# Up-projection weight loads of a mixture-of-experts stage moved from SyncE's queue to ScalarE's queue

## The chip, the cores and the metric

The kernel runs on one core of one Trainium2 chip. The metric is the device time of one execution in microseconds (us). Engines are named as in the profile: PE (TensorE), PEld (its weight loads), DVE (VectorE), ACT (ScalarE), POOL (GpSimd) and SP (SyncE). An engine's name with a q (SPq) means its sequencer, which issues DMA instructions. The core has 16 DMA engines, and every queue uses all of them.

## The reference, cut to what matters

One inference step of a two-layer hybrid decoder on 264 tokens (256 of a prompt, 8 of decoding), all in float32. Each layer first mixes tokens (pooling, differential attention, a state space), then runs a mixture of experts. For this change only the experts matter:

```
scores = sigmoid(t @ w_r)                      # 264 tokens, 64 experts, the best 8 per token
for each of 64 experts (wg, wu: 1024 x 256; wd: 256 x 1024; 1 MB each):
    a = silu(t @ wg) * (t @ wu)
    acc += gate[:, None] * (a @ wd)
shared = (silu(t @ sg) * (t @ su)) @ sd
```

## The kernel before, in words

**Tiling.** Before the expert loop the kernel sorts each expert's tokens into blocks of 64. Every expert has one block, and 32 spare blocks take the tokens beyond 64 of crowded experts. The loop has 96 steps: after every second expert comes one spare block. So 64 steps use weights whose address is known when the program is built ("main" steps), and 32 use weights that are found by an index ("spare" steps, numbers 2, 5, 8, 11 and so on). Spare blocks that no expert needs have an index out of bounds, and then no weights are read.

**Buffers.** Gate and up weights of a step share one slot `raw[n % 5]` of 2 MB, one half each. Down weights have 4 slots `dn`, the gathered token rows `xg` 4 buffers, the output rows `ytok` 4 buffers. A main step's gate, up and down loads have 1 MB each, in rows of 8 KB, and the semaphore of a slot counts 16 for each half.

**Order by engine in step n.** No planner is at work; each engine has a program written by hand, and semaphores tie them together.

- PE: `gate_up(n)` (line 1263, 32 matmuls), `turn_x(n+1)` (line 879, transposes of the gathered rows `xg`), `down(n-1)` (line 1276), `turn_act(n)` (line 879, input `scratch`). `turn_x` waits for the gather of its step.
- ACT: `copy_x(n+1)` (line 1474) moves the transposed rows out of PSUM, then it waits for `gu_made` of step n (the end of `gate_up(n)`), then silu (line 1498).
- DVE: the product with the up half (line 1853), the copy of the output rows (line 1859), the copy of the transposed activation (line 1863).
- SP: `gate_up(m)` waits until step m-5 has left the slot, then issues the gate half and the up half (line 642, one after the other); then `down(m-2)` waits for its slot and issues the down weights (line 657). Spare steps are skipped.
- POOL: waits for `turn_x(n+1)`, issues the gather of step n+4 (line 821); in a spare step's turn its gate and up loads (line 834); then waits for the output rows of step n-1, issues their scatter (line 828), and in a spare step's turn the down load (line 834). At n = 8 and 9 it also sends a small table to memory and back (`sgate`, `gflat`, line 696) and waits for the first of these to land. All that POOL issues goes through one queue, in order.

Of the kernel before, what the change touches and what calls it, by code (L numbers as in the profile page):

```python
# [25 lines left out]
P = 128  # L26
# [22 lines left out]
NE, TOPK, NG, TOPG = 64, 8, 8, 4  # L49
# [23 lines left out]
STEPS = [b for e in range(NE) for b in ([e, NE + e // 2] if e % 2 == 1 else [e])]  # L73
assert NE // 2 == SPARE and sorted(STEPS) == list(range(BLOCKS))
NSTEP = len(STEPS)
NRAW, NDOWN, NX, NY = 5, 4, 4, 4
# [117 lines left out]
def program(nc, a, out):  # L194
# [12 lines left out]
    def placed(name, of, first, shape, dt):  # L207

        return nc.alloc_sbuf_tensor_at(name, shape, dt, offset=places[of] + 4 * first)
# [4 lines left out]
    def sig(name, per_layer):  # L214
        return Signal(sem(name), per_layer)
# [123 lines left out]
    raw = [placed(f"raw{n}", of, first, [P, 2, SEG], F32) for n, (of, first) in enumerate(raw_at)]  # L339
# [132 lines left out]
    raw_loaded = [sig(f"raw_loaded{r}", 32 * len(MAIN_RAW[r])) for r in range(NRAW)]  # L472
# [58 lines left out]
    def _(sp):  # L531
        def columns(w, s):
            return w[:, 256 * s:256 * s + 256].rearrange("(k p) n -> p k n", p=P)

        def seg(t):
            return t.rearrange("p (k n) -> p k n", k=KD)
# [49 lines left out]
        def wide_fill(layer, f):  # L586
            ada, win = a["w_ada"][layer], a["w_in"][layer]
            if f < ADA_FIRST:
                w, s = ada, 2 * f
            elif f < ADA_FIRST + WIDE_IN:  # L590
                w, s = win, 2 * (f - ADA_FIRST)
            else:
                w, s = ada, 2 * (f - WIDE_IN)
            sp.wait_ge(wide_free, layer * WIDE_FILLS + f + 1)
            for j in range(2):
                sp.dma_start(seg(wide[:, f % 2, j]), columns(w, s + j)).then_inc(wide_loaded[f % 2], 16)
# [11 lines left out]
        for layer in range(DEPTH):  # L608
            wout = a["w_out"][layer]
            for f in range(0 if layer == 0 else 2, WIDE_OUT):  # L610
                if f == 2:
                    load_parameters(layer)
                wide_fill(layer, f)
            sp.wait_ge(wide_free, layer * WIDE_FILLS + WIDE_OUT + 1)
            for j in range(2):
                sp.dma_start(seg(wide[:, WIDE_OUT % 2, 0])[:, 4 * j:4 * j + 4],
                             columns(wout, 0)[:, 4 * j:4 * j + 4]).then_inc(wide_loaded[WIDE_OUT % 2], 16)
            for f in range(NARROW_SHARED):
                sp.wait_ge(narrow_free, layer * NARROW_FILLS + f + 1)
                sp.dma_start(seg(narrow[:, f % 2]), columns(wout, f + 1)).then_inc(narrow_loaded[f % 2], 16)  # L620

            sp.wait_ge(wide_free, layer * WIDE_FILLS + WIDE_SHARED + 1)
            for j, name in enumerate(("shared_w_gate", "shared_w_up")):
                sp.dma_start(seg(wide[:, 1, j]), a[name][layer].rearrange("(k p) n -> p k n", p=P)).then_inc(wide_loaded[1], 16)

            def gate_up(n):
                b = STEPS[n]
                if n == 0:
                    sp.wait_ge(attn_mixed.sem, attn_mixed.by(layer, 1))
                elif n == 1:  # L630
                    sp.wait_ge(ada_late.sem, ada_late.by(layer, WIDE_ADA - ADA_FIRST))
                    sp.wait_ge(ssm_mixed.sem, ssm_mixed.by(layer, 1))
                elif n == 2:
                    sp.wait_ge(out_first_used.sem, out_first_used.by(layer, 1))
                elif n == 3:
                    sp.wait_ge(hrows_stored.sem, hrows_stored.by(layer, 48))
                elif n == 4:
                    sp.wait_ge(sh_made.sem, sh_made.by(layer, 2))
                else:
                    sp.wait_ge(gu_made.sem, gu_made.by(layer, n - NRAW + 1))  # L640
                for j, name in enumerate(("exp_w_gate", "exp_w_up")):
                    sp.dma_start(raw[n % NRAW][:, j], a[name][layer, b].rearrange("(p k) n -> p (k n)", p=P))\
                        .then_inc(raw_loaded[n % NRAW].sem, 16)

            def down(n):
                b = STEPS[n]
                if n == 0:
                    sp.wait_ge(out_last_used.sem, out_last_used.by(layer, 1))
                elif n == 1:
                    sp.wait_ge(out_made.sem, out_made.by(layer, KD))  # L650
                elif n == 2:
                    sp.wait_ge(sh_down.sem, sh_down.by(layer, KD))
                elif n == 3:
                    sp.wait_ge(sh_made.sem, sh_made.by(layer, 2))
                else:
                    sp.wait_ge(down_made.sem, down_made.by(layer, n - NDOWN + 1))
                sp.dma_start(dn[n % NDOWN][:, :, :].rearrange("p j n -> p (j n)"),
                             a["exp_w_down"][layer, b].rearrange("(p j) n -> p (j n)", p=P))\
                    .then_inc(down_loaded[n % NDOWN].sem, 16)

            for n in range(NSTEP + 2):
                if n < NSTEP and STEPS[n] < NE:
                    gate_up(n)
                if n == 1:
                    sp.wait_ge(narrow_free, layer * NARROW_FILLS + NARROW_SHARED + 1)
                    sp.dma_start(narrow[:, 1].rearrange("p (k n) -> p k n", k=2),
                                 a["shared_w_down"][layer].rearrange("(k p) n -> p k n", p=P)).then_inc(narrow_loaded[1], 16)
                if n >= 2 and STEPS[n - 2] < NE:
                    down(n - 2)

            if layer + 1 < DEPTH:
                for f in range(2):
                    wide_fill(layer + 1, f)
            for r in range(NY):
                sp.wait_ge(y_scattered[r].sem, y_scattered[r].by(layer + 1, 0))
            ytok_k = yrows_k.rearrange("(t k) n -> t k n", k=TOPK)
            for g in range(4):
                for t in range(2):
                    sp.dma_start(ypart[t][g // 2][:, 2 * (g % 2):2 * (g % 2) + 2, :],
                                 ytok_k[P * t:P * t + P, 2 * g:2 * g + 2, :]).then_inc(y_loaded[g].sem, 16)  # L680
            sp.dma_start(ysam[:, :], yrows_k[TOPK * NP_:TOPK * T, :]).then_inc(ysam_loaded.sem, 16)

        yrows = projT[:, :, :].rearrange("p a b -> p (a b)")[:, 0:3 * D].rearrange("p (a b) -> p a b", a=3)
        for t in range(3):
            sp.wait_ge(last["copied"], 2 * t + 2)
            dst, n = (out["y_prompt"][0, P * t:P * t + P, :], P) if t < 2 else (out["y_sample"][:, 0, :], NS)
# [634 lines left out]
    def _(se):  # L1321
# [10 lines left out]
        for layer in range(DEPTH):  # L1332

            def W(s, k=1):
                se.wait_ge(s.sem, s.by(layer, k))
# [36 lines left out]
            for c in range(0, PROJ, 2):  # L1372
                W(proj_made, c + 1)
                act_(projT[:, c, :], ps[:, c % 4, 0:T], ACT.Copy).then_inc(proj_copied_a.sem, 1)
                if c % 4 == 2:

                    p = c // 4
# [9 lines left out]
            for n in range(4):  # L1387
                m = 512 if n < 3 else 256
# [79 lines left out]
            def copy_x(n):  # L1468
                W(x_turned, n + 1)
                if n == 0:  # L1470
                    W(table_made, 3)
                elif n >= 2:
                    W(gu_made, n - 1)
                act_(xTs[n % 2][:, :, :].rearrange("p k r -> p (k r)"), ps[:, n % 2, :], ACT.Copy).then_inc(x_copied.sem, 1)  # L1474
# [3 lines left out]
            for t in range(3):  # L1478
                n = P if t < 2 else NS
# [14 lines left out]
            for n in range(NSTEP):  # L1494
                if n + 1 < NSTEP:
                    copy_x(n + 1)
                W(gu_made, n + 1)
                act_(silu[:, n % 2, :], ps[:, 2 + n % 2, 0:128], ACT.Silu).then_inc(silu_ready.sem, 1)  # L1498
        se.wait_ge(x_ready.sem, DEPTH + 1)
        act_(hT[:, :, :], xT[:, :, :], ACT.Square).then_inc(squares.sem, 1)  # L1500
        se.wait_ge(var_ready.sem, var_ready.by(DEPTH, 1))
# [2 lines left out]
        for t in range(3):  # L1504
            n = P if t < 2 else NS
# [541 lines left out]
```

## Time and profile before

| | us |
|---|---|
| median of 3 runs (range) | 2146.23 (2140.99 to 2147.12) |
| the profiled execution, its own time | 2142.01 |
| its span | 2140.3 |
| expert loop of layer 0, from its first gate matmul | about 408 to 1033 |
| expert loop of layer 1, the same | about 1442 to 2070 |
| mean granted TensorE clock | 0.937 |

The page shows busy time by engine, DMA traffic by queue and groups of instructions. Times inside the span count from its start. q1 is the queue of SP's DMAs ("hardware_dynamic"), q0 that of POOL's ("software_dynamic"). A packet is one unit that a DMA engine moves: 8 KB at most here, and much less for a gather's row, for an index out of bounds or for a semaphore count. The landing time of an issue counts from its start to the arrival of its data. A granted clock of 1.00 is 2.4 GHz.

### The profile page before, as it was taken

The numbers are of one execution on the slowest core, as the hardware profiler recorded it, in microseconds if no ns is written. First come the engines' busy times: TensorE is split into PE (matmuls) and PEld (weight loads), VectorE is DVE, ScalarE is ACT, GpSimd is POOL, SyncE is SP. The second block draws the span as 40 slices with busy tenths as digits, with TensorE's granted clock in tenths as the row PEclk, the third lists the DMA queues.
The fourth block names the chain that finished last, engine by engine and source line by source line (L and its number), as shares of the span: only waits on it lengthen the run. The fifth ranks groups of instructions, "written<-read, shape, count | busy, mean of one in ns | idle before, by whom it ended". The sixth has DMA issues, their size and how long they took to land.

```text
span 2140.3 us, 28721 instructions
## 1 busy us (share of the span) xinstructions
PE 1908.3 (89%) x11519; PEld 1030.0 (48%) x11519; DVE 660.5 (31%) x1693; ACT 304.6 (14%) x705; POOL 695.3 (32%) x786
## 2 busy tenths in 40 slices
PE   5798977899999999999389897789899999999973
PEld 2473446544444444444248343564444444444432
DVE  1244483521111111111424628453111111111115
ACT  1120312111111111111011121121111111111101
POOL 2005010245444444444010410114444444444420
PEclk9898989999999999999689898889999999999995
DMA  7444435599999999998763454449999999999943
GB/s 230 150 157 161 158 100 208 236 414 380 360 351 343 365 362 351 352 355 318 241 221 107 132 197 138 158 166 402 413 364 355 354 354 347 345 357 349 351 162 141
DMA packets 216641, 588.91 MB, mean 275 GB/s; under 512 B 67705, under 2 KB 147277, under 8 KB 162622
## 3 DMA queue, kind: packets, MB, share of 16 engines
q1 hardware_dynamic: 149278, 507.35, 63.1%
q0 software_dynamic: 67232, 79.73, 11.0%
q8 instruction: 92, 1.51, 0.3%
q14 instruction: 39, 0.32, 0.0%
HBM read 775.20 MB, written 56.95 MB: 389 GB/s over the span
## 4 chain that ended last, share of the span: by engine, by line
PE 70%; issue 15%; DVE 8%; DMA 3%; ACT 1%; POOL 1%; POOLq 0%; SPq 0%; ACTq 0%; DVEq 0%
PE ps L1263 33%; PE ps L1276 16%; PE ps L879 8%; PE ps L923 4%; PE ps L1151 2%; DMA xg<-hrows,idx_x 2%; PE ps L1213 1%; PE ps L1031 1%; DMA ypart<-yrows_k 1%; PE ps L907 1%; DVE vbuf L1825 1%; PE ps L882 1%; PE ps L1190 1%; DVE scratch L1798 0%; PE ps L1056 0%
## 5 line engine op out<-in xcount | busy, mean ns | idle before, releaser
L1263 PE MATMUL ps<-raw,xTs 128*64 128x256 f32 x6144 | 742.0, 392 | 1.4 <-ACT xTs L1474 1.4
L1263 PEld LDWEIGHTS ps<-raw,xTs 128*64 128x64 f32 x6144 | 417.0, 135 | 258.8 <-issue 3.5
L1276 PE MATMUL ps<-dn,scratch 128*64 128x512 f32 x1536 | 373.0, 606 | 1.5 <-DVE scratch L1863 1.5
L828 POOL DMA_INDIRECT yrows_k<-ytok,idx_y x192 | 196.9, 1026 | 544.1 <-DVE ytok L1859 501.6
L1853 DVE TENSOR_TENSOR scratch<-scratch,ps 128x128 f32<-128x128 f32 x192 | 55.2, 287 | 860.7 <-ACT scratch L1498 860.7
L1474 ACT ACTIVATE xTs<-ps 128x512 f32<-128x512 f32 x192 | 114.6, 597 | 1126.0 <-PE ps L879 1126.0
L821 POOL DMA_INDIRECT xg<-hrows,idx_x x192 | 200.1, 1042 | 123.2 <-DVE idx_x L1950 65.2
L923 PE MATMUL ps<-wide,condT 128*9 128x256 f32 x768 | 187.0, 403 | 16.3 <-DMA wide<-in_w_ada 14.5
L1859 DVE COPY ytok<-ps 128x512 f32<-128x512 f32 x192 | 132.8, 691 | 156.5 <-PE ps L1276 156.5
L703 POOL TENSOR_TENSOR tick_p<-cst 1x1 f32<-1x1 f32 x32 | 6.8, 211 | 495.7 <-DVE scratch L1718 232.5
L1276 PEld LDWEIGHTS ps<-dn,scratch 128*64 128x64 f32 x1536 | 93.3, 136 | 144.6 <-issue 142.5
L879 PE MATMUL ps<-cst,xg 128*128 128x128 f32 x768 | 127.2, 289 | 18.3 <-DMA xg<-hrows,idx_x 18.3
L923 PEld LDWEIGHTS ps<-wide,condT 128*9 128x9 f32 x768 | 71.1, 95 | 126.6 <-issue 44.5
L970 PE MATMUL ps<-hT,wide 128*128 128x264 f32 x512 | 119.2, 397 | 13.9 <-DVE hT L1560 13.9
L879 PEld LDWEIGHTS ps<-cst,xg 128*128 128x128 f32 x768 | 81.1, 141 | 95.8 <-issue 75.0
L970 PEld LDWEIGHTS ps<-hT,wide 128*128 128x128 f32 x512 | 100.0, 196 | 32.4 <-issue 14.6
L879 PEld LDWEIGHTS ps<-cst,scratch 128*128 128x128 f32 x224 | 30.2, 138 | 162.0 <-DVE scratch L1853 154.7
L834 POOL DMA_INDIRECT dn<-in_exp_w_down,idx_w x64 | 65.2, 1018 | 22.6 <-issue 22.6
L879 PE MATMUL ps<-cst,scratch 128*128 128x128 f32 x224 | 70.2, 324 | 2.5 <-DVE scratch L1853 2.5
L834 POOL DMA_INDIRECT raw<-in_exp_w_gate,idx_w x64 | 63.8, 996 | 20.9 <-issue 18.9
L834 POOL DMA_INDIRECT raw<-in_exp_w_up,idx_w x64 | 63.8, 997 | 19.5 <-issue 19.5
L879 PE MATMUL ps<-cst,ysum 128*128 128x128 f32 x32 | 11.0, 447 | 62.4 <-DVE ysum L2003 62.4
(359 smaller groups left out, 1434.2 us busy)
## 6 DMA issues: line engine op xcount, KB each, us to landing
raw<-in_exp_w_gate SPq DMA_DIRECT2D x128, 1024.0 KB, 7.4
raw<-in_exp_w_up SPq DMA_DIRECT2D x128, 1024.0 KB, 9.9
dn<-in_exp_w_down SPq DMA_DIRECT2D x128, 1024.0 KB, 7.7
wide<-in_w_ada SPq DMA_DIRECT2D x48, 1024.0 KB, 7.8
wide<-in_w_in SPq DMA_DIRECT2D x16, 1024.0 KB, 6.9
ypart<-yrows_k SPq DMA_DIRECT2D x16, 1024.0 KB, 12.0
kbuf<-in_cache_k POOLq DMA_DIRECT2D x32, 256.0 KB, 3.0
vbuf<-in_cache_v POOLq DMA_DIRECT2D x32, 256.0 KB, 5.5
```

Of the source, the lines that this page charges most:

```text
L821: pool.indirect_dma_start(xg[n % NX][:, :], None, hrows.rearrange("t (h d) -> (t h) d", h=2), bass.IndirectOffsetOnAxis(ap=idx_x[:, b:b + ...
L828: pool.indirect_dma_start(yrows_k.rearrange("t (h d) -> (t h) d", h=2), bass.IndirectOffsetOnAxis(ap=idx_y[:, b:b + 1], axis=0), ytok[n % ...
L834: pool.indirect_dma_start(dst, None, a[name].rearrange(v, p=P), bass.IndirectOffsetOnAxis(ap=idx_w[:, o:o + 1], axis=0), bounds_check=P * ...
L879: return nc.tensor.transpose(dst, src, ident[0:n, 0:n])
L923: ins = mm(ps[0:NC, bank, 256 * j:256 * j + 256], condT[:, k, :], seg[:, k, :], start=k == 0, stop=k == KD - 1, skip_group_check=True)
L970: ins = mm(ps[:, c % 4, 0:T], w[:, k, P * (c % 2):P * (c % 2) + P], hT[:, k, :], start=k == 0, stop=k == KD - 1)
L1151: ins = mm(ps[:, c % 4, 0:T], w[:, k, P * (c % 2):P * (c % 2) + P], mixT[:, k, :], start=k == 0, stop=k == KD - 1)
L1263: ins = mm(ps[64 * h:64 * h + 64, 2 + n % 2, 0:256], xTs[n % 2][:, k % 4, 64 * (k // 4):64 * (k // 4) + 64], w[:, k, h], start=k == 0, sto ...
L1276: ins = mm(ps[64 * h:64 * h + 64, 5 + n % 2, :], actT[:, n % 2, 64 * j:64 * j + 64], dn[n % NDOWN][:, j, 512 * h:512 * h + 512], start=j = ...
L1474: act_(xTs[n % 2][:, :, :].rearrange("p k r -> p (k r)"), ps[:, n % 2, :], ACT.Copy).then_inc(x_copied.sem, 1)
L1853: tt(act[:, n % 2, :], silu[:, n % 2, :], ps[:, 2 + n % 2, 128:256], ALU.mult).then_inc(act_ready.sem, 1)
L1859: cp(ytok[n % NY][:, :], ps[:, 5 + n % 2, :]).then_inc(y_copied.sem, 1)
```

## The change

For steps m from 5 on, the up half of a main step's weights is no longer issued by SP but by ACT, in iteration n = m-5, behind the silu of step n. That silu has already waited for `gu_made` of step n, which is what frees the slot. Steps 0, 1, 3 and 4 keep both halves on SP. Gate halves, down weights, and all loads of the spare steps stay where they were. The semaphore counts stay as they were. 60 loads of 1 MB per layer move, 120 in all.

```
                 else:
                     sp.wait_ge(gu_made.sem, gu_made.by(layer, n - NRAW + 1))
-                for j, name in enumerate(("exp_w_gate", "exp_w_up")):
+                for j, name in enumerate(("exp_w_gate", "exp_w_up") if n < NRAW else ("exp_w_gate",)):
                     sp.dma_start(raw[n % NRAW][:, j], a[name][layer, b].rearrange("(p k) n -> p (k n)", p=P))\
                         .then_inc(raw_loaded[n % NRAW].sem, 16)
...
                 W(gu_made, n + 1)
                 act_(silu[:, n % 2, :], ps[:, 2 + n % 2, 0:128], ACT.Silu).then_inc(silu_ready.sem, 1)
+                m = n + NRAW
+                if m < NSTEP and STEPS[m] < NE:
+                    se.dma_start(raw[m % NRAW][:, 1], a["exp_w_up"][layer, STEPS[m]].rearrange("(p k) n -> p (k n)", p=P))\
+                        .then_inc(raw_loaded[m % NRAW].sem, 16)
```

## Rows read from the trace of the kernel before

**Rows 1.** The page, part 1: busy us, share of the span, instructions.

```profile
PE 1908.3 (89%) x11519; PEld 1030.0 (48%) x11519; DVE 660.5 (31%) x1693; ACT 304.6 (14%) x705; POOL 695.3 (32%) x786
```

**Rows 2.** Busy time in stretches: PE, PEld, DVE, ACT, POOL; PE clock, DMA share, GB/s.

```profile
700.00:800.00 100.00, 100.00 (x692) 49.03 (x690) 18.80 (x48) 12.08 (x32) 45.63 (x45) 1.00 0.95 359
...
1516.00:1536.00 20.00, 17.70 (x107) 8.36 (x109) 3.18 (x8) 2.29 (x6) 9.06 (x10) 0.86 1.02 414
```

**Rows 3.** Timeline of one step in mid-loop: start, us, engine, line [idle before <-releaser].

```profile
706.21 1.94 PE L1276 MATMUL ps<-dn,scratch 128*64 128x512 f32 x8
...
708.34 3.85 PE L1263 MATMUL ps<-raw,xTs 128*64 128x256 f32 x32
...
712.59 0.43 SPq L642 DMA_DIRECT2D raw<-in_exp_w_up  x1
...
712.80 0.60 ACT L1474 ACTIVATE xTs<-ps 128x512 f32<-128x512 f32 x1 [5.72 <-PE ps L879]
...
713.30 0.27 ACT L1498 ACTIVATE scratch<-ps 128x128 f32<-128x128 f32 x1
```

**Rows 4.** DMA issues of 1700 to 1900 us: count, median us to landing.

```profile
xg<-hrows,idx_x POOLq DMA_INDIRECT x31, 4.9
```

**Rows 5.** Timeline, layer 0: gather of step 8 issued, turn_x(8), turn_x(11).

```profile
438.96 1.02 POOL L821 DMA_INDIRECT xg<-hrows,idx_x  x1 [0.30 <-issue]
...
458.91 0.66 PE L879 MATMUL ps<-cst,xg 128*128 128x128 f32 x4
...
478.60 0.66 PE L879 MATMUL ps<-cst,xg 128*128 128x128 f32 x4 [0.15 <-DMA xg<-hrows,idx_x]
```

**Rows 6.** DMA issues of 438.9 to 440 us (layer 0): us to landing.

```profile
xg<-hrows,idx_x POOLq DMA_INDIRECT x1, 19.6
```

**Rows 7.** Timeline, layer 1: gather of step 8; turn_x of 8, 11, 14; down after 11.

```profile
1473.07 1.02 POOL L821 DMA_INDIRECT xg<-hrows,idx_x  x1 [0.30 <-issue]
...
1493.03 0.66 PE L879 MATMUL ps<-cst,xg 128*128 128x128 f32 x4
...
1518.30 1.11 PE L879 MATMUL ps<-cst,xg 128*128 128x128 f32 x4 [5.74 <-DMA xg<-hrows,idx_x]
1519.34 3.09 PE L1276 MATMUL ps<-dn,scratch 128*64 128x512 f32 x8
...
1539.75 0.66 PE L879 MATMUL ps<-cst,xg 128*128 128x128 f32 x4 [0.31 <-DMA xg<-hrows,idx_x]
```

**Rows 8.** DMA issues of 1473 to 1474 us (layer 1): us to landing.

```profile
xg<-hrows,idx_x POOLq DMA_INDIRECT x1, 19.9
```

**Rows 9.** DMA queues, 422 to 458.6 us: packets, MB, share of 16 engines.

```profile
q1 hardware_dynamic: 1365, 10.00, 66.0%
```

**Rows 10.** DMA queues, 458.6 to 478.6 us, the same columns.

```profile
q1 hardware_dynamic: 929, 6.77, 81.9%
q0 software_dynamic: 931, 1.45, 19.6%
```

**Rows 11.** DMA queues, 1493 to 1518.3 us, the same columns.

```profile
q1 hardware_dynamic: 930, 6.76, 64.8%
q0 software_dynamic: 928, 3.75, 36.6%
```

**Rows 12.** DMA issues of 454.9 to 455.4 us (layer 0): us to landing.

```profile
dn<-in_exp_w_down SPq DMA_DIRECT2D x1, 1024.0 KB, 15.7
```

**Rows 13.** DMA queues, 458.6 to 471 us, columns as in rows 9.

```profile
q1 hardware_dynamic: 527, 3.86, 75.3%
```

**Rows 14.** DMA issues of 1512 to 1514 us (layer 1): us to landing.

```profile
raw<-in_exp_w_gate SPq DMA_DIRECT2D x1, 1024.0 KB, 18.4
raw<-in_exp_w_up SPq DMA_DIRECT2D x1, 1024.0 KB, 21.7
```

**Rows 15.** DMA queues, 1518.3 to 1531 us, columns as in rows 9.

```profile
q1 hardware_dynamic: 544, 3.97, 75.7%
```

**Rows 16.** DMA issues of 1524.9 to 1525.5 us (layer 1): us to landing.

```profile
xg<-hrows,idx_x POOLq DMA_INDIRECT x1, 14.8
```

More of the change, by code:

```diff
@@ L640, in gate_up @@
                     sp.wait_ge(gu_made.sem, gu_made.by(layer, n - NRAW + 1))
-                for j, name in enumerate(("exp_w_gate", "exp_w_up")):
+                for j, name in enumerate(("exp_w_gate", "exp_w_up") if n < NRAW else ("exp_w_gate",)):
                     sp.dma_start(raw[n % NRAW][:, j], a[name][layer, b].rearrange("(p k) n -> p (k n)", p=P))\
@@ L1498, in _ @@
                 act_(silu[:, n % 2, :], ps[:, 2 + n % 2, 0:128], ACT.Silu).then_inc(silu_ready.sem, 1)
+                m = n + NRAW
+                if m < NSTEP and STEPS[m] < NE:
+                    se.dma_start(raw[m % NRAW][:, 1], a["exp_w_up"][layer, STEPS[m]].rearrange("(p k) n -> p (k n)", p=P))\
+                        .then_inc(raw_loaded[m % NRAW].sem, 16)
         se.wait_ge(x_ready.sem, DEPTH + 1)
```

## The prediction, made before the changed kernel ran

> **What bounds the kernel now.** I read the busy shares first: PE is busy for 89% of the span, no other engine for a third of that [rows 1]. Next the busy time in stretches. In mid-loop PE is busy for 100 of 100 us at full clock, and the DMA engines for 95% [rows 2]. So in mid-loop PE sets the pace and a faster load buys nothing; but the DMA engines have only 5% to spare. Early in each loop the picture turns. In 1516 to 1536 us the DMA engines are full (1.02), PE idles for 2.3 us of 20 and its granted clock is 0.86 of 2.4 GHz, so part of that stretch ran at the 1.2 GHz level [rows 2]. There the first spare blocks read real weights, so 3 MB are wanted in every step and not in two of three.
>
> Then the timeline: what ends PE's waits there? Not a weight load. It is always the gather of token rows, which is POOL's: 0.15 us before turn_x(11) of layer 0 [rows 5], 5.74 us before turn_x(11) and 0.31 us before turn_x(14) of layer 1 [rows 7]. Others only just make it. The gather of step 8 was issued at 438.96 us, landed 19.6 us later at 458.56, and was used at 458.91, 0.35 us to spare [rows 5, 6]. In layer 1 it was issued at 1473.07, landed at 1492.97 and was used at 1493.03, 0.06 us to spare [rows 7, 8]. In mid-loop a gather takes 4.9 us [rows 4], so some 15 us are in reserve there. **The resource to watch is the turn that POOL's queue gets on the DMA engines in the first 15 steps of each loop.**
>
> Last the DMA queues. In 20.0 us of layer 0 SP's queue moved 929 packets and POOL's 931 [rows 10]; in 25.3 us of layer 1 it was 930 and 928 [rows 11]. POOL's packets are much smaller (1.45 MB against 6.77). So with work in both queues, the engines take one packet of each in turn, whatever its size, and each small packet of POOL's waits for an 8 KB packet of SP's. One packet of SP's costs an engine 66.0% of 36.6 us over 1365/16 = 85 packets, or 0.283 us [rows 9].
>
> The Trainium skill, "DMA: Bandwidth & Descriptors", section "Queues, rings and completion order", says that each DMA engine goes round robin between the queue rows that have work, a packet at a time, and that SP and ACT own a row each; by that rule three rows would share the turns after the change. The trace agrees for two queues; no row here shows three.
>
> **The change, part by part.** Each layer has 60 moved loads.
>
> *SP loses an issue* of 0.43 us [rows 3]. SP waits for PE in every step, so nothing is gained: 0.
>
> *ACT gains an issue.* At SP's price that is 0.43 us, behind the silu that ends at 713.57. Behind it on ACT stands only the next copy_x, and ACT idled 5.72 us before that [rows 3]. Cost 0 as long as the issue takes less than 5 us; without that cover it would be 60 x 0.43 = 26 us per layer.
>
> *The up half starts later*: at about 713.6 in place of 712.6, 1 us. It is needed five steps less the 3.85 us of a gate_up after its slot is free [rows 3]; a step is (478.60 - 0.15 - 458.91)/3 = 6.5 us [rows 5], so that is 28.7 us. In the fullest stretch an up load took 21.7 us [rows 14]. Cost 0, and in a queue of its own it will land sooner than that.
>
> *The turns at the DMA engines.* This is the term that counts. In the full stretches the up halves now have their own turn, so POOL's queue gets one packet in three instead of one in two whenever all three have work. The engines are full either way, so a gather that lands later does so by just the extra weight packets that were moved ahead of it. That is bounded by what SP's queue still held at that moment before.
>
> Layer 0, step 8: the down load issued in 454.9 to 455.4 landed 15.7 us later at about 470.7 [rows 12], and from 458.6 to 471 SP's queue moved 527/16 = 33 packets per engine [rows 13]. So at most 33 x 0.283 = 9.3 us can be moved ahead. The other bound: only the up halves' third goes ahead, 3.1 us. How far does it go? Until then each queue had 85 turns. SP's new queue gets two thirds of 85 + 33 = 118 packets, or 79, fewer than its 85 turns, and the up queue the other 39, so both are nearly empty by then, except for the load just issued (9 packets). I take 33 - 9 = 24 packets, 6.8 us, less the 0.35 us to spare: 6.4 us. By turn_x(11) it can't be much more, since the same weights can go ahead only once. A wait of this length also drops the clock: after the 5.74 us wait the transposes took 1.11 us instead of 0.66 and the down matmuls 3.09 [rows 7] instead of 1.94 [rows 3], 1.6 us together. Layer 0: +8.0 us, bounds 2.8 and 12.2 (with two drops).
>
> Layer 1, turn_x(11), already late: SP's queue held the gate load, which landed 18.4 us after 1512.60 [rows 14], and the up load behind it. From 1518.3 to 1531, the gate's landing, 544/16 = 34 packets passed [rows 15], and with the up half 43, 12.2 us. The third alone is 4.1 us. Some of the last 27 of them, issued within the last 10 us, will not have gone; I leave 12 and take 31: +8.8 us. The drop of the clock is already in the time of before; one more bounds it at 13.8.
>
> The gather of step 14 is issued late, because POOL waits for its small table to land in the same slow queue. It took 14.8 us and was 0.31 us late [rows 7, 16]. If up loads add 6 packets x 0.283 = 1.7 us to each 6.5 us, the same turns last 1/(1 - 0.26) = 1.35 times as long, +5.2 us. But the weight queues are short by then. Bounds 0 and 5.2 in each layer, I take 2 each: +4.
>
> Sum: 8.0 + 8.8 + 4 = 20.8 us, bounds 6.9 and 36.4. The profiled execution took 2142.01 us (2140.3 of span, 1.7 around it), so it would take 2162.8. The median of the runs lies 4.2 us higher, and I forecast against the median: 2146.2 + 20.8 = **2167**.
>
> **The rivals.** *A, no change (0.12).* ACT's loads could share the turn of SP's queue. Then POOL keeps every second packet, no gather moves, and since the three full streams carry the same bytes the time stays at 2146. For it: PE is full in mid-loop and the moved issue is hidden. Against it: nothing in the rows ties two issuing engines to one turn; turns go by queue. The Trainium skill, "DMA: Bandwidth & Descriptors", section "Rules for kernel authors", says that spreading DMAs over SP, ACT and GpSimd does not help bandwidth and only saves issue time; read alone, that gives 2146 here, as no issue time is on the path.
>
> *B, faster (0.05).* A third stream could keep the engines fuller. The place is 1456 to 1518 us: to land the late gather 5.7 us sooner in 62 us, the rate must rise by about 10% above the 414 GB/s of [rows 2], from which point the waits are gone. They are worth 0.15 + 5.74 + 0.31 + 1.6 = 7.8 us: 2138. Against it: the share there is already 1.02.
>
> *C, much slower (0.07).* The longer queue of POOL's hurts in mid-loop too, where 5% of the DMA time is free, or ACT's issue blocks for over 5 us. The gather would have to grow from 4.9 to some 20 us; no row points to it. If it took 0.5 us in each of 150 steps: 2146 + 21 + 75 = 2242.
>
> **How the numbers follow.** The forecast has 0.76. What a measurement of this kernel can tell from no change is about 0.3%, 6.4 us. The forecast's own range is 2153 to 2183. The range given reaches down over case A: 2145 to 2183, which leaves out B, C and a little of the tail. Slower by over 0.3%: 0.76 less 0.03 for its low end, plus 0.07, gives 0.80. Same: 0.12 + 0.03 + 0.02 of B, whose whole gain hardly exceeds the bound: 0.17. Faster: 0.03.
>
> **What would show it.** One more hardware queue appears, with 120 loads of 1 MB. In the first 60 us of a loop POOL's queue moves clearly fewer packets than SP's and ACT's together, some 40% of all. Up loads land within 10 us there. Gathers of steps 8 to 11 take over 22 us, and PE waits for them in both layers, 6 us or more in layer 0. In mid-loop a step stays at 6.5 us. ACT's issue takes about 0.4 us and nothing waits for it. I am wrong if POOL's queue keeps half of the packets, if PE's waits for gathers don't grow, or if mid-loop steps grow.

## The result and the profile after

The changed kernel takes 2161.89 us in the median (2154.36 to 2165.5, 8 runs) against 2142.26 us before on the same chip: ratio 1.0084, 95% interval 1.0066 to 1.0102. It is slower, by about 18 us. The profiled execution took 2165.49 us (span 2163.8), 23.5 us more than the one before; it is one of the slowest of the eight.

The page of the changed kernel, part 1 and the DMA queues (packets, MB, share of 16 engines); the first line answers to [rows 1]:

```profile
PE 1920.7 (89%) x11519; PEld 1036.1 (48%) x11519; DVE 661.5 (31%) x1693; ACT 304.6 (14%) x705; POOL 694.7 (32%) x786
...
q1 hardware_dynamic: 131998, 381.52, 48.7%
q10 hardware_dynamic: 17280, 125.84, 14.1%
q0 software_dynamic: 67232, 79.73, 11.0%
```

The new queue q10 is ScalarE's, with 120 loads of 1 MB. The number of packets in all is that of before (216641). Nothing was added; something is served in another order.

Where did the time go? Not into mid-loop. The stretches view of 700 to 800 us, columns as in [rows 2]:

```profile
700.00:800.00 100.00, 100.00 (x694) 49.20 (x692) 18.83 (x48) 11.55 (x31) 47.59 (x47) 1.00 0.94 353
```

PE is still busy without a gap at full clock. The timeline of the first steps, `turn_x` of steps 6 to 9 of layer 0, answers to [rows 5]:

```profile
446.38 0.66 PE L879 MATMUL ps<-cst,xg 128*128 128x128 f32 x4
...
454.60 0.66 PE L879 MATMUL ps<-cst,xg 128*128 128x128 f32 x4 [1.67 <-DMA xg<-hrows,idx_x]
...
469.24 1.11 PE L879 MATMUL ps<-cst,xg 128*128 128x128 f32 x4 [8.07 <-DMA xg<-hrows,idx_x]
...
478.07 0.65 PE L879 MATMUL ps<-cst,xg 128*128 128x128 f32 x4
```

The first is step 6, in time. Step 7 waits 1.67 us for its gather and step 8 waits 8.07 us. From step 8 to step 9 it takes 8.83 us instead of 6.49: that is the lower clock after the wait, 2.3 us. In layer 1, `turn_x` of steps 7, 8, 9, 11 and 12 answers to [rows 7]:

```profile
1500.84 0.66 PE L879 MATMUL ps<-cst,xg 128*128 128x128 f32 x4
1515.62 1.11 PE L879 MATMUL ps<-cst,xg 128*128 128x128 f32 x4 [8.22 <-DMA xg<-hrows,idx_x]
1523.61 0.66 PE L879 MATMUL ps<-cst,xg 128*128 128x128 f32 x4
...
1540.01 1.12 PE L879 MATMUL ps<-cst,xg 128*128 128x128 f32 x4 [3.36 <-DMA xg<-hrows,idx_x]
1549.32 0.65 PE L879 MATMUL ps<-cst,xg 128*128 128x128 f32 x4
```

What this costs in all is read between `turn_x(0)` and `turn_x(12)` of each layer. The changed kernel, `turn_x` of steps 0 and 12 of layer 0 and of step 0 of layer 1 (step 12 of layer 1 is above):

```profile
407.06 1.11 PE L879 MATMUL ps<-cst,xg 128*128 128x128 f32 x4 [6.03 <-DMA xg<-hrows,idx_x]
...
497.53 0.65 PE L879 MATMUL ps<-cst,xg 128*128 128x128 f32 x4
...
1455.12 1.12 PE L879 MATMUL ps<-cst,xg 128*128 128x128 f32 x4 [6.04 <-DMA xg<-hrows,idx_x]
```

The kernel before, steps 0 and 12 of layer 0, then of layer 1:

```profile
406.66 1.11 PE L879 MATMUL ps<-cst,xg 128*128 128x128 f32 x4 [6.04 <-DMA xg<-hrows,idx_x]
...
485.08 0.66 PE L879 MATMUL ps<-cst,xg 128*128 128x128 f32 x4
...
1440.70 1.11 PE L879 MATMUL ps<-cst,xg 128*128 128x128 f32 x4 [6.06 <-DMA xg<-hrows,idx_x]
...
1526.40 0.66 PE L879 MATMUL ps<-cst,xg 128*128 128x128 f32 x4
```

In layer 0 the changed kernel needs 497.53 - 407.06 = 90.47 us, where the one before needed 485.08 - 406.66 = 78.42: **+12.05 us**. In layer 1 it is 1549.32 - 1455.12 = 94.20 against 1526.40 - 1440.70 = 85.70, +8.50, and before there was still a wait of 0.31 to come: **+8.2 us**. Together 20.2 us. The 3.3 us that are left of the profiled difference lie outside these two stretches (2.0 of them in the stage between the loops), and the medians differ by 19.6.

The DMA queues in two stretches of 4 us of layer 0, 446 to 450 and 450 to 454 us, columns as in [rows 9]:

```profile
q1 hardware_dynamic: 80, 0.63, 38.1%
q10 hardware_dynamic: 77, 0.62, 37.4%
q0 software_dynamic: 80, 0.41, 24.7%
...
q1 hardware_dynamic: 88, 0.60, 36.3%
q10 hardware_dynamic: 88, 0.60, 36.1%
q0 software_dynamic: 87, 0.49, 29.8%
```

This is the cause in six lines. With work in all three queues, each moves the same number of packets. POOL's queue had every second packet before [rows 10, 11]; now it has every third, and every packet of its own waits for two of 8 KB.

Equal counts alone could also come from turns of a whole load, which gives each engine 8 rows and one semaphore count. The packets' own records settle it. They don't name the DMA engine, but a packet can be linked to the one that ended within 12 ns of its start. In the kernel before, from 1493 to 1518.3 us, 1792 of 1840 packets linked in this way follow one of the other queue. In the changed kernel, from 450 to 454 us, 233 of 247 follow in the order SyncE, ScalarE, POOL. A turn is one packet. The gather of step 8, in the DMA issues of 439.4 to 440 us, answers to [rows 6]:

```profile
xg<-hrows,idx_x POOLq DMA_INDIRECT x1, 29.8
```

It took 29.8 us where it had taken 19.6. While PE waited, ScalarE's queue ran dry: from 462 to 466 us it moved nothing, and POOL's moved more packets than SyncE's, which still had work:

```profile
q1 hardware_dynamic: 170, 1.23, 73.6%
q0 software_dynamic: 205, 0.43, 28.1%
```

SyncE's queue was empty soon after (6 packets from 470 to 474 us). So weights had been fetched ahead of what PE needed next.

### The profile page after: what moved, and what is told of

The parts are those of the page before. It is cut to its first block, busy times and chain, and to the rows that moved or that the text cites. A ratio compares the mean times of both kernels' runs of the same rounds, so it can differ in the third digit from the quotient of the medians.

```text
span 2163.8 us, 28721 instructions
## 1 busy us (share of the span) xinstructions
PE 1920.7 (89%) x11519; PEld 1036.1 (48%) x11519; DVE 661.5 (31%) x1693; ACT 304.6 (14%) x705; POOL 694.7 (32%) x786
## 2 busy tenths in 40 slices
DMA packets 216641, 588.91 MB, mean 272 GB/s; under 512 B 67705, under 2 KB 147277, under 8 KB 162622
## 4 chain that ended last, share of the span: by engine, by line
PE 70%; issue 14%; DVE 7%; DMA 5%; ACT 1%; POOL 1%; POOLq 0%; SPq 0%; ACTq 0%; DVEq 0%
PE ps L1263 32%; PE ps L1276 16%; PE ps L879 8%; PE ps L923 4%; DMA xg<-hrows,idx_x 3%; PE ps L1151 3%; PE ps L1213 1%; PE ps L1031 1%; DMA ypart<-yrows_k 1%; PE ps L907 1%; PE ps L882 1%; PE ps L1190 1%; DVE scratch L1802 0%; PE ps L1056 0%; POOLq L725 0%
## 5 line engine op out<-in xcount | busy, mean ns | idle before, releaser
L834 POOL DMA_INDIRECT raw<-in_exp_w_gate,idx_w x64 | 63.7, 996 | 20.8 <-issue 18.9
```

The source lines that it names most:

```text
L834: pool.indirect_dma_start(dst, None, a[name].rearrange(v, p=P), bass.IndirectOffsetOnAxis(ap=idx_w[:, o:o + 1], axis=0), bounds_check=P * ...
```

## The experiments

All ratios are against the kernel before on the same chip. The chips differ by up to 0.6% (the kernel before had medians of 2142 to 2154 us), so only ratios are compared.

### Is it the queue or the moment of the issue?

e1 leaves the up half with SyncE, but issues it behind the same silu:

```
                 for j, name in enumerate(("exp_w_gate", "exp_w_up")):
+                    if j == 1 and n >= NRAW:
+                        sp.wait_ge(silu_ready.sem, silu_ready.by(layer, n - NRAW + 1))
                     sp.dma_start(raw[n % NRAW][:, j], a[name][layer, b]...
```

> The up half stays in SyncE's queue, but is issued behind the same silu, about 1 us later than before. Theory of the turns (three busy queues leave POOL's one packet in three): two queues as before, so the time of before, 2138 to 2148 us, PE waits for gathers of about 6 us in all (0.15 + 5.74 + 0.31 before). Rival 'the later issue costs': the time of the changed kernel, about 2160 us.

Measured: 2144.26 us, ratio 1.0002 (0.9993 to 1.0012), with a wait of 5.89 us before turn_x(11) of layer 1 as in [rows 7]. The up half leaves 1.37 us after the gate half there (0.37 us before, 0.59 us in the changed kernel), and nothing measurable is lost.

### Is it ScalarE's issue, or the number of busy queues?

e2 moves everything that SyncE loads in the loop to ScalarE; SyncE keeps the gate and up loads below step 5 and the down loads below step 4:

```
-                if m < NSTEP and STEPS[m] < NE:
-                    se.dma_start(raw[m % NRAW][:, 1], a["exp_w_up"]...
+                if m < NSTEP and STEPS[m] < NE:
+                    for j, name in enumerate(("exp_w_gate", "exp_w_up")):
+                        se.dma_start(raw[m % NRAW][:, j], a[name]...
+                m = n - 1 + NDOWN
+                if n >= 1 and m < NSTEP and STEPS[m] < NE:
+                    W(down_made, n)
+                    se.dma_start(dn[m % NDOWN]..., a["exp_w_down"]...
```

> From step 5 (down: 4) on gate, up and down loads are all issued by ScalarE, none by SyncE: ScalarE issues three times as many loads as in the change, but only two queues are busy. Theory of the turns: POOL's queue gets every second packet again, the time of before, 2138 to 2150 us. Rival 'an issue on ScalarE costs' or 'ScalarE's queue is served ahead of POOL's': 2160 us or more, with up to three times the loss of the change (2200 us).

Measured: 2141.99 us, ratio 0.9991 (0.9981 to 1.0). The DMA queues of e2 in 1493 to 1518.3 us (layer 1), the stretch of [rows 11]:

```profile
q10 hardware_dynamic: 929, 6.77, 64.8%
q0 software_dynamic: 928, 3.74, 36.5%
```

That is [rows 11] with q10 in q1's place. ScalarE issues three times as many loads as in the change, and nothing is lost: two busy queues, one packet each in turn. The wait before turn_x(11) of layer 1 is 5.80 us, as before.

i1 is e2 with the down loads left on SyncE (the lines from `m = n - 1 + NDOWN` on taken out, `down` as before):

> As e2, but the down loads stay on SyncE: ScalarE issues gate and up, so three queues are busy again and ScalarE issues a third less than in e2, which cost nothing. Theory of the turns: the loss is back, ratio 1.006 to 1.012. Rival 'only the up halves' own place matters' or 'what ScalarE issues matters': no loss, as in e2, ratio 0.998 to 1.002.

Measured: 2165.76 us, ratio 1.0069 (1.0045 to 1.0093). The waits in its timeline, first layer 0, then layer 1:

```profile
467.14 1.11 PE L879 MATMUL ps<-cst,xg 128*128 128x128 f32 x4 [8.74 <-DMA xg<-hrows,idx_x]
...
1516.65 1.12 PE L879 MATMUL ps<-cst,xg 128*128 128x128 f32 x4 [7.02 <-DMA xg<-hrows,idx_x]
...
1555.27 1.12 PE L879 MATMUL ps<-cst,xg 128*128 128x128 f32 x4 [4.08 <-issue]
```

What ended the last of these waits the profile does not show. ScalarE issues fewer loads than in e2, and the loss is back with the third queue. With gate and up moved it is about as large as with up alone.

### Where in the loop is it lost?

e3 moves the up loads only from step 24 on, e4 only for steps below 24:

```
-("exp_w_gate", "exp_w_up") if n < NRAW else ("exp_w_gate",)
+("exp_w_gate",) if n >= 24 else ("exp_w_gate", "exp_w_up")           # e3
+("exp_w_gate",) if NRAW <= n < 24 else ("exp_w_gate", "exp_w_up")    # e4
```

ScalarE's condition is narrowed to the same steps (not shown).

> The up loads move to ScalarE only from step 24 on, where PE was busy for 100% of the time. Theory of the turns: nothing is late there, the time of before, 2138 to 2148 us. Rival 'the loss is spread over the loop': 72 of 91 steps keep the move, so about 0.8 of the loss, 2157 us.

Measured: 2145.03 us, ratio 1.001 (1.0 to 1.0019).

> The up loads move to ScalarE only for steps 6 to 23 of each layer, 12 loads per layer. Theory of the turns: the whole loss of the change, 2155 to 2166 us, with PE waits of about 8 us before turn_x(8) in both layers. Rival 'the loss is spread over the loop': about 0.2 of the loss, 2146 us.

Measured: 2160.01 us, ratio 1.0076 (1.0059 to 1.0093). A move of 12 loads per layer gives the loss of all 60, within the intervals. PE's waits for gathers in e4 are those of the change (8.72 us in layer 0, 8.30 and 3.87 us in layer 1), in e3 those of before (5.58 and 0.35 us in layer 1). In mid-loop the third queue costs at most some 4 us (the interval of e3 goes from 0 to 4).

### Is the gather the only load that comes late?

f1 (the kernel before) and f2 (the changed one) have 6 gather buffers instead of 4, two of them in free scratch space, so each gather is issued two steps earlier:

```
-NRAW, NDOWN, NX, NY = 5, 4, 4, 4
+NRAW, NDOWN, NX, NY = 5, 4, 6, 4
```

> The kernel before with 6 gather buffers instead of 4, so that each gather is issued two steps (13 us) earlier; queues as before. Theory: the gathers are the only loads that come late, so the waits before turn_x(11) and turn_x(14) go and with them 7.8 us: 2133 to 2137 us. Rival 'the stretch is short of DMA bandwidth, whatever the order': a weight load becomes the late one and the time stays at 2143.

> The changed kernel with 6 gather buffers. Theory: the up loads still take every third packet, but a gather has 13 us more than the 8 to 10 us that it was late, so the loss of the change goes: 2133 to 2140 us, ratio below 1. Rival 'the third queue costs in itself': the loss of the change stays, 2150 us or more.

Measured: f1 2151.62 us, ratio 1.0009 (1.0 to 1.0018); f2 2168.92 us, ratio 1.0086 (1.0072 to 1.01). Both expectations of the theory failed, and the times that the rivals gave came. The waits of PE in f2's timeline, two of layer 0 and two of layer 1 (line 1265 is the gate and up matmul, 1278 the down matmul):

```profile
468.06 5.33 PE L1265 MATMUL ps<-raw,xTs 128*64 128x256 f32 x32 [3.86 <-DMA raw<-in_exp_w_up,idx_w]
...
486.14 3.68 PE L1278 MATMUL ps<-dn,scratch 128*64 128x512 f32 x8 [5.67 <-issue]
...
1520.90 6.21 PE L1265 MATMUL ps<-raw,xTs 128*64 128x256 f32 x32 [5.50 <-DMA raw<-in_exp_w_up,idx_w]
...
1538.32 3.68 PE L1278 MATMUL ps<-dn,scratch 128*64 128x512 f32 x8 [4.13 <-issue]
```

No gather is late any more. The up weights of a spare block are, and then a down matmul waits. The profile names no releaser for it, but the semaphore events of the trace do: 0.09 us before each of these down matmuls the last count of a spare block's down load arrives, and that semaphore has no further event for over 24 us. f1 has the same two kinds of wait in layer 1, 1.97 us for spare up weights and 2.58 us for spare down weights. The spare weights come through POOL's queue as well. So what is late is the whole of POOL's queue, not the gather; an earlier gather only lets its neighbour in the queue be the late one.

### Does a turn go by packets or by bytes?

g1 (before) and g2 (changed) issue each 1 MB load of a main step as two loads with rows of 4 KB:

```
+                    for u in range(2):
+                        sp.dma_start(raw[n % NRAW][:, j, 1024 * u:1024 * u + 1024],
+                                     a[name][layer, b].rearrange("(p k) n -> p (k n)", p=P)[:, 1024 * u:1024 * u + 1024])
...
```

The down load is halved in the same way, and the semaphore counts are doubled (not shown).

> The kernel before, with each 1 MB load of a main step's weights issued as two loads of rows of 4 KB (same bytes, twice the packets, half as long each). Theory of the turns by packet: each of POOL's packets waits for 4 KB instead of 8 KB, so gathers in the full stretch take clearly less than 20 us and the waits go: 2133 to 2138 us. Rival 'turns go by bytes or time': no change, 2143 us; rival 'small packets waste bandwidth': slower, 2150 us or more.

> The changed kernel with the same rows of 4 KB. Theory: POOL's packet waits for two packets of 4 KB, which is one of 8 KB again, so about the time of before, 2136 to 2148 us. Rival 'turns go by bytes or time': the loss of the change stays, 2160 us.

Measured: g1 2147.35 us, ratio 0.9989 (0.9979 to 0.9998); g2 2154.57 us, ratio 1.0023 (1.0014 to 1.0032), where f2 on the same chip had 1.0086. Halving the weights' packets takes away about three quarters of the loss against the kernel before. Against g1, the third queue still costs 7 us, 0.34% in place of 0.84%: g2 did not come back to the time of before, as the theory had it. The counts show that turns go by packets. g2 from 452 to 456 us with three queues busy, and g1 from 440 to 450 us with two:

```profile
q1 hardware_dynamic: 196, 0.71, 43.9%
q10 hardware_dynamic: 196, 0.71, 43.8%
q0 software_dynamic: 198, 0.22, 15.5%
...
q0 software_dynamic: 433, 2.47, 61.0%
q1 hardware_dynamic: 437, 1.59, 39.5%
```

The packets are equal in number and the bytes are not, in g1 with more of them on POOL's side. In g1 and g2 no gather is late. But g1 gains 2 us, not 8, since now a load of the other side comes late. Its timeline in layer 1, a down matmul whose releaser the profile does not name:

```profile
1511.88 3.38 PE L1279 MATMUL ps<-dn,scratch 128*64 128x512 f32 x8 [3.87 <-issue]
```

The semaphore events name it again: the last count of a down load of SyncE's arrives 0.09 us before. g2 has three such waits, of 3.05 us in layer 0 and of 4.21 and 3.36 us in layer 1, each ended by a down load of SyncE's in the same way.

### Can the turns be balanced so that nothing is late?

h1 is g1 with the down loads left at 8 KB; h2 is h1 with 6 gather buffers; h3 is g1 with 6 gather buffers.

> The kernel before with rows of 4 KB for the gate and up loads of the main steps and rows of 8 KB for down (g1 had 4 KB for all three, and then a down load came 3.9 us late in layer 1). Theory (the full stretch has almost no bandwidth to spare, and the turns only decide which load is the late one): POOL's loads gain, the down loads lose less than in g1, so little or nothing is late, 4 to 8 us less than before, ratio 0.996 to 0.998. Rival 'the waits are fixed by the bytes alone': 0.999 as g1.

> As h1, with 6 gather buffers as in f1. Theory: gathers can't be late any more, but two more of them stand ahead of the spare weights in POOL's queue, which were late in f1; with the shorter rows these have more turns, so no waits at all, ratio 0.996. Rival: the waits only move, 0.999 or more.

> As g1 (all main weight loads in rows of 4 KB), with 6 gather buffers. Theory: gathers were not late in g1, so more buffers give nothing and the down load stays late, ratio 0.999 to 1.000.

Measured: h1 ratio 0.999 (0.9981 to 1.0), h2 1.0008 (0.9999 to 1.0016), h3 1.0013 (1.0004 to 1.0022). The theory's 0.996 to 0.998 for h1 and 0.996 for h2 did not come, and h3 lies a little above its 0.999 to 1.000. h1 still shows waits in layer 1 before two down matmuls:

```profile
1507.03 1.94 PE L1278 MATMUL ps<-dn,scratch 128*64 128x512 f32 x8 [1.14 <-issue]
...
1529.90 3.43 PE L1278 MATMUL ps<-dn,scratch 128*64 128x512 f32 x8 [2.81 <-issue]
```

Both end 0.09 us after the last count of a down load of SyncE's, and so do the waits of h2 (1.55 and 3.31 us) and h3 (3.77 us). So in layer 1 a better share for POOL only moves the wait. That the stretch is close to short of bandwidth as a whole is argued from this; no run shows how much is missing. The order of service can lose 18 us, and in these trials it could win back some 2, hardly clear of the noise. No version was found that beats the kernel before by more.

## Why the prediction was right, and where not

**Right, by its own steps.** The forecast was 2167 with the range 2145 to 2183; measured were 2161.9. The sum said +20.8 us, and the loops of the profiled run show 20.2 (medians 19.6). Four of the five us by which the forecast is high come from its base, the median of three runs (2146.2); that of eight is 2142.3.

- *What bounds it.* POOL's queue in the first 15 steps of each loop: shown by e3 and e4, which part at step 24, and by where the waits stand, steps 7 to 11.
- *One packet of each queue in turn, also with three.* Shown by the counts 88, 88 and 87, by the packets that follow each other, and by e2 and i1, in which the number of busy queues decides and not what ScalarE issues. The rule of the Trainium skill ("DMA: Bandwidth & Descriptors", "Queues, rings and completion order"), a round robin between the queues with work, agrees with these counts; the packet that it gives, some 9 to 17 descriptors before the switch, does not, since here the queue changes after one row. Rival A, "ScalarE's loads share SyncE's turn", is out. The same page's "Rules for kernel authors" says that spreading loads over issuing engines doesn't help; here it did harm, by 0.84%.
- *A packet, whatever its size.* Shown by the counts and bytes of g1 and g2.
- *Costs put at nothing.* ScalarE's issue takes 0.34 us and its next copy still follows 5.72 us of idle time, as before:

```profile
447.07 0.60 ACT L1474 ACTIVATE xTs<-ps 128x512 f32<-128x512 f32 x1 [5.72 <-PE ps L879]
447.08 0.34 ACTq L1501 DMA_DIRECT2D raw<-in_exp_w_up  x1
447.56 0.27 ACT L1498 ACTIVATE scratch<-ps 128x128 f32<-128x128 f32 x1
```

  e2, with three issues in that place, shows the cover is ample, and e1 that the later issue costs nothing.
- *Mid-loop untouched* (rival C): a step is 6.49 us as before.

**Off in size.** In layer 0 the term was 8.0 us and measured 12.05. Waits of 1.67 + 8.07 = 9.7 us stand against 6.4 for step 8, and a clock drop of 2.3 against 1.6. The step that failed is "I take 33 - 9 = 24 packets". From `turn_x(0)` to the landing of the gather of step 8, SyncE's queue moved 1362 packets before; SyncE's and ScalarE's together moved 1846 in the changed kernel. That is 30 more per engine, nearly all of the 33: during PE's wait no new weights are asked for (SyncE issues nothing from 461.2 to 474.0 us), and what is queued drains. The bound of 9.3 us was the better estimate.

In layer 1 the term was 8.8 (8.2 measured), but its parts are others. The wait stands 8.22 us long already at step 8, where the prediction had looked at step 11, and 3.36 us at step 11. Together the waits grew by 5.5 us only (11.6 against 6.05). The other 2.7 us are the clock, which dropped twice (1.5 and 2.8 us against 1.6 before); the prediction had put that at nothing and all 8.8 us on the wait. That its term fits is luck. The two terms for the gather of step 14, 2 us each, were wrong: it was late in neither layer. The total fits in part because these errors offset each other.

**Wrong in what it showed as proof.** Up loads were to land within 10 us in the full stretch. The load issued at 447.08 took 11.5 us: ScalarE's queue was still moving its data from 454 to 458 us, and its last semaphore count came at 458.58.

```profile
q1 hardware_dynamic: 75, 0.59, 35.4%
q0 software_dynamic: 77, 0.58, 35.0%
q10 hardware_dynamic: 72, 0.52, 31.5%
```

(The view of DMA issues gives 18.0 us for this load, but it counts the semaphore that both halves share, which is full when the gate half has landed too.) Two up loads in a row, 6.5 us apart, fill a queue that gets a third of the packets.

The sign for POOL's share failed as it was worded. In the first 60 us of a loop its queue was to move some 40% of the packets, clearly fewer than the other two together. From 407.1 to 467.1 us it moved 2127 of 3895, 55%, and in layer 1 2130 of 3928, 54%. The reason is the stretch: in the first 18 us of it POOL's queue has the engines nearly to itself. From 426 to 469.3 us it is 1347 of 3127, 43%, and a third where all three queues have work. Read by the letter, "I am wrong if POOL's queue keeps half of the packets" would have spoken against a mechanism that holds.

**Wrong in the carrier.** "It is always the gather" was read off the waits of before. The gather is only the first item of POOL's queue that is missed; f2 showed that the spare blocks' weights behind it are as late, up and down, and f1 the same on a smaller scale. The forecast did not suffer, since it counted the packets of the queue, not those of the gather. But the remedy that one would draw from it, more gather buffers, gains nothing.

**Open.** What ended the wait of 4.08 us in i1, and how much bandwidth the full stretch lacks. Whether issuing some weights later would shorten the waits of the kernel before was not tried.

## What to carry to other kernels

When the DMA engines are full, count packets by queue in stretches of a few us. If the counts are equal, the queues share by turns, and a further queue takes from every other one; it hurts most the one with small packets and near deadlines. Moving loads to an idle engine's queue cost next to nothing here where the queues were short (e3), and 18 us where they had a backlog (e4). And look at who stands next in the queue before giving one of its loads more lead.

## What the runs showed of the hardware that was not expected

ScalarE's DMA issue does not wait for the activation ahead of it in the program: it began at 447.08 us, and the silu it stands behind at 447.56 (lines above). So the up load left 0.6 us after the gate load's issue (446.49), not the 1.4 us that the prediction took. The order was still safe, since the wait for `gu_made` stands ahead of both.
